# Product-key routing and one-hot batches in a two-layer decoder: where they stand, how they are laid out

## The chip, the cores and the metric

The kernel runs on one core of one Trainium2 chip. Its engines work side by side, each through its own queue of instructions in order: TensorE (PE, with its weight loads as PEld), VectorE (DVE), ScalarE (ACT), GpSimd (POOL) and SyncE (SP), which here only issues DMAs. They wait for each other by semaphores. The metric is the time on the device in microseconds (us), the median of several runs.

## What is computed

256 tokens of width 2048 pass two layers. Each ends with a PEER feed-forward part, which is what the change is about. Float32 throughout.

```python
def peer_ffn(h, w_q, keys_1, keys_2, expert_u, expert_v):
    q = (h @ w_q).reshape(b, s, PEER_HEADS, 2, PEER_HALF)          # 8 heads x 2 halves x 128
    s1 = jnp.einsum('bshd,hkd->bshk', q[..., 0, :], keys_1)        # 128 keys
    s2 = jnp.einsum('bshd,hkd->bshk', q[..., 1, :], keys_2)
    v1, i1 = lax.top_k(s1, 16)
    v2, i2 = lax.top_k(s2, 16)
    cand_sc = v1[..., :, None] + v2[..., None, :]                  # 256 candidates
    cand_id = i1[..., :, None] * 128 + i2[..., None, :]
    top_sc, pos = lax.top_k(cand_sc, 16)
    ids, g = cand_id[pos], softmax(top_sc)                         # 128 experts of 16384 per token
    act = gelu(expert_u[ids] @ h)
    return (g * act) @ expert_v[ids]
```

## The kernel before

**No gather.** The kernel runs over all 16384 experts. In the first pass of a layer 128 tiles of `expert_u` (128 experts each) are multiplied with the tokens and give the activations. In the second pass 128 tiles of `expert_v` are multiplied with activation times weight, where the weight of an expert that a token did not choose is zero. These dense weights come from the routing: for each token a matmul of one-hots, `hot2` (128 choices x second index) with `hot1g` (128 choices x first index, times g), gives a 128 x 128 block. g is split in two float16 parts, so each token has two matmuls of 128 columns (`build_w`, lines 1267 and 1268), and a batch of eight tokens has sixteen. There are 32 batches in a layer.

**Units.** All weights come through one stream of units of 128 x 2048 floats (1 MB). SP loads them into four raw slots (`load`, L348). ACT copies each half of a unit into `hi` (`split_hi`, L473), and DVE or POOL subtracts and gives `lo` (`split_lo`, L684 and L437), in a ring of four halves. Thus the hi of unit n+2 waits until TensorE is through with the same half of unit n. `gpsimd_takes` gives POOL one half of four, and three of four in the stretch of the routing. TensorE multiplies hi with both parts of the tokens (L1168) and lo with one (L1167), 32 matmuls for a unit of the projection or the first pass (`unit_a`), 24 of 512 columns for one of the second (`out_unit`, L1296, L1298, L1300). `unit_a` can run a piece of work, `middle`, between the two halves of a unit.

**Order on the engines.** It is written out by hand. A layer's PEER part is 16 units of projection (`routing`), 128 of the first pass (`peer`, index j) and 128 of the second (index t).
- In the projection DVE does for each unit u: the lo of unit u+2, the sum of unit u (`sum_halves`, L689, which frees the PSUM bank that unit u+2 needs), and the top 16 of unit u-1 (`route_unit`), whose keys product TensorE makes in the middle of unit u. Every second `route_unit` also makes the 256 candidates (L793) and their top 16.
- Tiles j = 0 to 6 of the first pass hold the last of these, then the decoding of the chosen places into indices (`decode`, L824, and `sum_places`, L834) and the softmax; at j = 7 TensorE transposes the selections and DVE stores them (`store_selections`).
- From j = 10 on, one tile in three carries a batch: DVE makes its one-hots behind the sum of tile j (L874 and L876, 24 instructions), TensorE multiplies them in the middle of tile j+1, and ACT copies the result into `w_stage` ahead of its work for tile j+2 (`stage_weights`, L557). Eight batches fill a stage, which SP stores in eight pieces of 512 KB, one every second tile (the last eight one in each tile).
- In the second pass four tiles are a group. For the next group DVE multiplies activation and weight (`weigh`, L882) at step i = 1, ACT copies this into `wa` (`coefficients_hi`, L566) at i = 2, and DVE subtracts (`coefficients_lo`, L886) at i = 3. Each stands on DVE behind the lo of unit t+2. TensorE waits for L886 ahead of the group's first matmul.

## Time and profile before

| | |
|---|---|
| median of 3 runs | 4781.25 us (4781.08 to 4782.48) |
| the profiled execution | 4780.19 us, its span 4778.5 us |
| TensorE busy | 4114.4 us, 86% of the span |
| VectorE, ScalarE, GpSimd busy | 48%, 37%, 20% |
| mean granted TensorE clock | 0.926 of full speed |
| DMA | 823 MB, mean 172 GB/s |

Matmuls are pipelined, so the starts of two of them give the pace, and busy time does not. "Idle before" is the time in which the engine had nothing to run, and the arrow names what ended it; "issue" is where the profile names nobody, as when the engine that was waited for had ended just before. A clock of 1.00 is 2.4 GHz, of 0.50 is 1.2; a window that holds both shows a value between.

### The profile page before, as it was taken

The page shows a single profiled execution, that of the slowest core. Times are in us where ns is not written, and L with a number is a line of the kernel's source. Part 1 is how long each engine was busy: PE and PEld are TensorE (multiplying, and loading weights), DVE is VectorE, ACT ScalarE, POOL GpSimd, SP SyncE. Part 2 cuts the span into 40 slices and gives each one's busy share as a digit, 9 for nine tenths or more (in the row PEclk, how much of TensorE's full clock was granted, in tenths as well). Part 3 has the DMA queues.
Part 4 walks back from the last instruction along what each step waited for, and adds up shares of the span by engine and source line. Part 5 has one row for each costly group of instructions (what it writes and reads, how often), then busy time and mean ns, then how long its engine had stood idle before and what let it go on. Part 6 is the DMA issues. An engine that isn't in the chain of part 4 may idle for free.

```text
span 4778.5 us, 50402 instructions
## 1 busy us (share of the span) xinstructions
PE 4114.4 (86%) x20142; PEld 3419.8 (72%) x20142; DVE 2312.9 (48%) x4301; ACT 1776.4 (37%) x2124; POOL 957.7 (20%) x422
## 2 busy tenths in 40 slices
PE   7988887788779999999898887887788998888887
PEld 6867766667667877777676776766667776666666
DVE  4444775555554444444446477555555433333333
ACT  3344333333334444434433423333333333333333
POOL 1232441111111222222110143111111111111111
PEclk9999998888889999999988999988888999999999
DMA  4533443455456766666432434445555765555553
GB/s 181 185 128 115 150 147 137 158 166 160 153 179 203 256 223 220 224 225 224 172 122 82 150 129 149 141 150 163 167 161 168 215 223 191 187 194 183 187 190 136
DMA packets 279163, 823.34 MB, mean 172 GB/s; under 512 B 146064, under 2 KB 178832, under 8 KB 195216
## 3 DMA queue, kind: packets, MB, share of 16 engines
q1 hardware_dynamic: 278496, 816.96, 50.0%
q8 instruction: 160, 2.62, 0.2%
q10 hardware_dynamic: 432, 3.15, 0.2%
q14 instruction: 75, 0.61, 0.0%
HBM read 750.84 MB, written 69.21 MB: 172 GB/s over the span
## 4 chain that ended last, share of the span: by engine, by line
PE 78%; DVE 9%; issue 9%; ACT 3%; POOL 0%; DMA 0%; DVEq 0%; SPq 0%; ACTq 0%; POOLq 0%
PE bank L1168 24%; PE bank L1167 12%; PE bank L1296 10%; PE bank L1300 10%; PE bank L1298 10%; PE bank L1188 2%; PE bank L1190 2%; DVE lo L684 2%; PE bank L1189 2%; ACT hi L473 2%; DVE wa L886 1%; PE bank L1267 1%; PE bank L1268 1%; DVE match L824 1%; PE bank L1170 1%
## 5 line engine op out<-in xcount | busy, mean ns | idle before, releaser
L473 ACT ACTIVATE hi<-raw 128x1024 fp32r<-128x1024 f32 x1294 | 1366.2, 1059 | 2440.4 <-PE bank L1168 1225.1
L684 DVE TENSOR_TENSOR lo<-raw,hi 128x1024 fp32r<-128x1024 f32 x919 | 1139.1, 1240 | 2077.4 <-ACT hi L473 2077.0
L1168 PE MATMUL bank<-act_t,hi 128*128 128x512 f32 x5120 | 1868.2, 411 | 23.2 <-DVE stage L689 17.7
L437 POOL TENSOR_TENSOR lo<-raw,hi 128x1024 fp32r<-128x1024 f32 x375 | 916.3, 2444 | 3746.5 <-ACT hi L473 3746.5
L1167 PE MATMUL bank<-act_t,lo 128*128 128x256 f32 x4800 | 1403.9, 292 | 0.0
L1168 PEld LDWEIGHTS bank<-act_t,hi 128*128 128x128 f32 x5120 | 990.1, 198 | 243.0 <-DVE stage L689 20.6
L1167 PEld LDWEIGHTS bank<-act_t,lo 128*128 128x128 f32 x4800 | 961.0, 200 | 13.5
L1296 PE MATMUL bank<-hi,wa 128*128 128x512 f32 x2048 | 672.3, 410 | 141.0 <-DVE wa L886 134.9
L1298 PE MATMUL bank<-lo,wa 128*128 128x512 f32 x2048 | 662.1, 405 | 0.0
L1300 PE MATMUL bank<-hi,wa 128*128 128x512 f32 x2048 | 661.5, 405 | 0.0
L1296 PEld LDWEIGHTS bank<-hi,wa 128*128 128x128 f32 x2048 | 393.5, 195 | 260.9 <-DVE wa L886 161.8
L1298 PEld LDWEIGHTS bank<-lo,wa 128*128 128x128 f32 x2048 | 397.1, 194 | 98.8
L1300 PEld LDWEIGHTS bank<-hi,wa 128*128 128x128 f32 x2048 | 396.3, 193 | 98.3
L1267 PE MATMUL bank<-hot1g,hot 128*128 128x128 f16 x512 | 112.5, 306 | 324.0 <-issue 313.8
L1267 PEld LDWEIGHTS bank<-hot1g,hot 128*128 128x128 f16 x512 | 72.7, 143 | 342.6 <-issue 342.6
L876 DVE TENSOR_SCALAR hot1g<-iota,sel_t 128x128 f16<-128x128 f16 x1024 | 275.6, 316 | 0.0
L689 DVE TENSOR_REDUCE stage<-bank 128x256 f32<-128x512 f32 x256 | 175.8, 687 | 177.9 <-PE bank L1168 174.3
L546 ACT ACTIVATE stage<-stage 128x256 f32<-128x256 f32 x256 | 105.7, 413 | 314.9 <-DVE stage L689 314.9
L874 DVE TENSOR_SCALAR hot<-iota,sel_t 128x128 f16<-128x128 f16 x512 | 198.5, 388 | 0.0
L1188 PE MATMUL bank<-hi,act_t 128*128 128x512 f32 x448 | 176.3, 394 | 3.7 <-DVE act_t L733 1.9
L1189 PE MATMUL bank<-lo,act_t 128*128 128x512 f32 x448 | 175.7, 392 | 0.0
L1190 PE MATMUL bank<-hi,act_t 128*128 128x512 f32 x448 | 175.6, 392 | 0.0
(208 smaller groups left out, 2348.4 us busy)
## 6 DMA issues: line engine op xcount, KB each, us to landing
raw<-in_stream SPq DMA_DIRECT2D x647, 1024.0 KB, 4.8
act_rows<-stage SPq DMA_DIRECT2D x64, 512.0 KB, 6.7
w_rows<-w_stage SPq DMA_DIRECT2D x64, 512.0 KB, 7.5
acts<-act_rows SPq DMA_DIRECT2D x64, 512.0 KB, 5.7
w_part<-w_rows SPq DMA_DIRECT2D x64, 512.0 KB, 6.7
x_res<-in_x SPq DMA_DIRECT2D x2, 1024.0 KB, 6.0
keys_sb<-in_keys ACTq DMA_DIRECT2D x2, 1024.0 KB, 4.8
out<-xn SPq DMA_DIRECT2D x2, 1024.0 KB, 4.0
```

The costliest lines, as they stand in the source:

```text
L437: pool.tensor_tensor(lo[:, s, :], raw[:, n0 % RAW_SLOTS, j * HALF:(j + 1) * HALF], hi[:, s, :].bitcast(F32), ALU.subtract).then_inc(lo_rea ...
L473: act.activation(hi[:, s, :], raw[:, slot, j * HALF:(j + 1) * HALF], ACT.Copy).then_inc(hi_ready[s], 1)
L684: dve.tensor_tensor(lo[:, s, :], raw[:, n0 % RAW_SLOTS, j * HALF:(j + 1) * HALF], hi[:, s, :].bitcast(F32), ALU.subtract).then_inc(lo_read ...
L876: ins = dve.tensor_scalar(hot1g[:, b % 2, t, w, :], iota[:], sel_t[:, 0, tok:tok + 1], sel_t[:, 2 + w, tok:tok + 1], ALU.is_equal, ALU.mult)
L1167: mm(ps[:, 0:S], w_lo, act_t[:, kt, 0, :], start=False, stop=False, skip_group_check=True)
L1168: ins = mm(ps[:], w_hi, act_t[:, kt, :, :].rearrange("p w t -> p (w t)"), start=first, stop=last)
L1188: mm(o, a_hi, w_hi, start=(kt == 0), stop=False)
L1189: mm(o, a_hi, w_lo, start=False, stop=False)
L1190: ins = mm(o, a_lo, w_hi, start=False, stop=(kt == kt_end - 1))
L1296: mm(o[:], a_hi, hi[:, s, at], start=first, stop=False)
L1298: mm(o[:], a_hi, lo[:, s, at], start=False, stop=False)
L1300: ins = mm(o[:], a_lo, hi[:, s, at], start=False, stop=last)
```

## The change

The routing is dealt over projection and first pass: TensorE's keys products stand in the middle of units i = 2, 3, 5, 6, 8, 9, ... (i counts from the projection's first unit), DVE takes the top 16 of the same unit's keys in these and the top 16 of a head's candidates in every third (`route_step`), then decoding takes units 26 to 39, and the selections are turned at unit 41 (j = 25). For this all sixteen projected units are kept (`pq_t`).

Batches begin at j = 26, two in every three tiles. The one-hots of eight tokens are made by four instructions on 1024 elements of float16, with the token as the innermost dimension. TensorE uses them three tiles later, reading each token's columns with a step of eight elements, and ACT stages the result one tile after that. Pieces of a stage are stored one per tile. GpSimd keeps its three halves of four up to j = 26. In the second pass `weigh`, `coefficients_hi` and `coefficients_lo` stand at i = 0, 1 and 2.

```diff
-BATCH_TILE = 10
-BATCH_STEP = 3
+BATCH_TILE = 26
+BUILD_LAG = 3
...
-TURN_TILE = 7
-EXP_TILE = 3
+ROUTE_AT = 2
+DECODE_AT = ROUTE_AT + 3 * 8
+TURN_AT = 41
+EXP_TILE = 12
...
-    b, off = divmod(tile - BATCH_TILE, BATCH_STEP)
-    return b if off == 0 and 0 <= b < BATCHES else None
+    three, r = divmod(tile - BATCH_TILE, 3)
+    b = 2 * three + r
+    return b if r < 2 and 0 <= b < BATCHES else None
+
+
+def last_batch_tile(f):
+
+    return BATCH_TILE + 3 * (FLUSH * (f + 1) - 1) // 2
...
-        pq_t = place("pq_t", 8, [P, 2, S])
+        pq_t = place("pq_t", 48, [P, 2 * PEER_HEADS, S])
...
+        g_full = place("g_full", 66, [P, S])
+        iota_rep = place("iota_rep", 67, [P, NKEYS, BATCH], F16)
+        hot1 = place("hot1", 69, [P, NKEYS, BATCH], F16)
+        hot2 = place("hot2", 71, [P, 2, NKEYS, BATCH], F16)
+        hot1g = place("hot1g", 75, [P, 2, 2, NKEYS, BATCH], F16)
...
-            busy = any(U0[f"wq{k}"] + LEAD <= n0 < U0[f"peer{k}"] + TURN_TILE + 3 + LEAD for k in range(2))
+            busy = any(U0[f"wq{k}"] + LEAD <= n0 < U0[f"peer{k}"] + BATCH_TILE + LEAD for k in range(2))
             return s >= 1 if busy else s == HALF_SLOTS - 1
...
-                    f, at = divmod(done - BATCH_TILE - 4, BATCH_STEP * FLUSH)
-                    piece, odd = divmod(at, 2 if f < FLUSHES else 1)
-                    if 1 <= f <= FLUSHES and piece < PIECES and odd == 0:
-                        store_weights(layer, f - 1, piece)
+                    f = next((f for f in range(FLUSHES) if 0 <= done - last_batch_tile(f) - BUILD_LAG - 3 < PIECES), None)
+                    if f is not None:
+                        store_weights(layer, f, done - last_batch_tile(f) - BUILD_LAG - 3)
...
-                    if batch_at(j - 2) is not None:
-                        stage_weights(batch_at(j - 2))
+                    b = batch_at(j - BUILD_LAG - 1)
+                    if b is not None:
+                        stage_weights(b)
                     split_hi(base + j + LEAD)
-                    if j == TILES - GROUP + 2:
+                    if j == TILES - GROUP + 1:
                         coefficients_hi(0)
                     gelu(j)
...
-                    if i == 2 and g + 1 < GROUPS:
+                    if i == 1 and g + 1 < GROUPS:
                         coefficients_hi(g + 1)
...
                 dve.wait_ge(c_full, idx + 1)
+                steps.sync()
                 top16(lambda c: ps_c[idx % 2][:, c * P:(c + 1) * P], lambda c: top_v[:, c, h, half, :],
...
+
+            def route_pairs(h):
+
                 steps.sync()
                 top16(lambda c: cand[:, c, :], lambda c: sel_v[:, c, h, :], lambda c: sel_p[:, c, h, :],
...
-                dve.tensor_copy(sel_t[:, 0:2, :].rearrange("p w t -> p (w t)"), ps_c[c0 % 2][:]).then_inc(c_free, 1)
+                dve.tensor_copy(i1_t[:], ps_c[c0 % 2][:, 0:S])
+                dve.tensor_copy(i2_t[:], ps_c[c0 % 2][:, S:2 * S]).then_inc(c_free, 1)
...
-                steps.do(dve.tensor_copy(g_half[:], g_full[:]))
-                steps.sync()
-                steps.do(dve.tensor_copy(sel_t[:, 2, :], g_half[:]))
-                steps.sync()
-                steps.do(dve.tensor_tensor(sel_t[:, 3, :], g_full[:], sel_t[:, 2, :], ALU.subtract))
-                steps.sync()
+                steps.do(dve.tensor_copy(g_parts[:, 0, :], g_full[:]))
+                steps.sync()
+                steps.do(dve.tensor_tensor(g_parts[:, 1, :], g_full[:], g_parts[:, 0, :], ALU.subtract))
+                steps.sync()
+
+            def route_step(layer, i):
+
+                n, r = divmod(i - ROUTE_AT, 3)
+                if 0 <= n < PEER_HEADS:
+                    if r < 2:
+                        route_unit(layer, 2 * n + r)
+                    else:
+                        route_pairs(n)
+                n = i - DECODE_AT
+                if n == 0:
+                    start_decoding(layer)
+                elif 1 <= n <= 12:
+                    w, r = divmod(n - 1, 6)
+                    if r < 4:
+                        decode(w, 4 * r, 4 * r + 4)
+                    else:
+                        sum_places(w, r - 4)
+                elif n == 13:
+                    finish_softmax(layer)
+                elif i == TURN_AT:
+                    store_selections(layer)
...
-                    if layer * BATCHES + b >= 2:
-                        dve.wait_ge(w_full, layer * BATCHES + b - 1)
-                    for t in range(BATCH):
-                        tok = BATCH * b + t
-                        dve.tensor_scalar(hot2[:, b % 2, t, :], iota[:], sel_t[:, 1, tok:tok + 1], None, ALU.is_equal)
-                        for w in range(2):
-                            ins = dve.tensor_scalar(hot1g[:, b % 2, t, w, :], iota[:], sel_t[:, 0, tok:tok + 1],
-                                                    sel_t[:, 2 + w, tok:tok + 1], ALU.is_equal, ALU.mult)
+                    done = layer * BATCHES + b
+                    tok = slice(BATCH * b, BATCH * (b + 1))
+                    if done >= 2:
+                        dve.wait_ge(w_full, done - 1)
+                    dve.tensor_tensor(hot2[:, b % 2, :, :], iota_rep[:],
+                                      i2_t[:, tok].unsqueeze(1).to_broadcast([P, NKEYS, BATCH]), ALU.is_equal)
+                    if done > 0:
+                        dve.wait_ge(hots_ready, done)
+                    dve.tensor_tensor(hot1[:], iota_rep[:], i1_t[:, tok].unsqueeze(1).to_broadcast([P, NKEYS, BATCH]),
+                                      ALU.is_equal).then_inc(hot1_ready, 1)
+                    dve.wait_ge(hot1_ready, done + 1)
+                    for w in range(2):
+                        ins = dve.tensor_tensor(hot1g[:, b % 2, w, :, :], hot1[:],
+                                                g_parts[:, w, tok].unsqueeze(1).to_broadcast([P, NKEYS, BATCH]), ALU.mult)
                     ins.then_inc(hots_ready, 1)
...
-                        if i == 1:
+                        if i == 0:
                             weigh(g + 1)
-                        elif i == 3:
+                        elif i == 2:
                             coefficients_lo(g + 1)
...
                     sum_tile(j)
...
+                    route_step(layer, 2 * PEER_HEADS + j)
                     if batch_at(j) is not None:
                         one_hots(batch_at(j))
...
+                steps.do(dve.tensor_copy(iota_rep[:], iota[:].unsqueeze(2).to_broadcast([P, NKEYS, BATCH])))
                 for u in range(2 * PEER_HEADS):
                     split_lo(w0 + u + LEAD)
-
-                    if C0[f"wq{layer}"] + u - 1 > 0:
-                        dve.wait_ge(c_full, C0[f"wq{layer}"] + u - 1)
                     unit_done(dve, w0 + u)
-                    sum_halves(pq_t[:, u % 2, :], a0 + u)
-                    if u >= 1:
-                        route_unit(layer, u - 1)
+                    sum_halves(pq_t[:, u, :], a0 + u)
+                    route_step(layer, u)
...
+            def key_unit(i):
+
+                n, r = divmod(i - ROUTE_AT, 3)
+                return 2 * n + r if r < 2 and 0 <= n < PEER_HEADS else None
...
-                        mm(o, hot2[:, b % 2, t, :], hot1g[:, b % 2, t, 0, :], start=True, stop=False)
-                        ins = mm(o, hot2[:, b % 2, t, :], hot1g[:, b % 2, t, 1, :], start=False, stop=True)
+                        mm(o, hot2[:, b % 2, :, t], hot1g[:, b % 2, 0, :, t], start=True, stop=False)
+                        ins = mm(o, hot2[:, b % 2, :, t], hot1g[:, b % 2, 1, :, t], start=False, stop=True)
...
+                    i, b = 2 * PEER_HEADS + j, batch_at(j - BUILD_LAG)
+                    middle = None
+                    if key_unit(i) is not None:
+                        middle = lambda u=key_unit(i): keys_product(layer, u)
+                    elif i == TURN_AT:
+                        middle = turn_selections
+                    elif b is not None:
+                        middle = lambda b=b: build_w(b)
+                    unit_a(base + j, a0 + j, middle=middle)
```

## Rows read from the trace of the kernel before

**Rows 1.** Windows: us; busy (x instructions) PE PEld DVE ACT POOL; PEclk, DMA, GB/s
```profile
686.80:1489.60 802.80, 640.72 (x3596) 556.75 (x3595) 423.95 (x1008) 290.57 (x353) 117.75 (x50) 0.89 0.50 159
...
1520.00:1560.00 40.00, 40.00 (x228) 34.75 (x227) 17.20 (x18) 17.47 (x22) 9.53 (x4) 1.00 1.01 274
...
1614.00:2363.00 749.00, 723.87 (x3068) 572.75 (x3069) 304.88 (x254) 300.11 (x286) 153.63 (x64) 1.00 0.61 221
...
3875.40:4763.00 887.60, 777.81 (x3068) 612.84 (x3069) 303.45 (x254) 298.27 (x285) 151.28 (x63) 0.93 0.51 183
```
**Rows 2.** Waits of the whole span: total us, times, longest us
```profile
PE bank L1267 <- issue: 313.8, 62, 5.1
...
PE bank L1296 <- DVE wa L886: 134.9, 62, 3.5
```
**Rows 3.** Timeline of TensorE, one batch of layer 0: start, length, idle before
```profile
801.10 0.27 PE L1267 MATMUL bank<-hot1g,hot 128*128 128x128 f16 x1 [5.11 <-issue]
...
802.72 0.56 PE L1167 MATMUL bank<-act_t,lo 128*128 128x256 f32 x1
```
**Rows 4.** Timeline of VectorE: first and last one-hots of that batch
```profile
796.04 0.25 DVE L874 TENSOR_SCALAR hot<-iota,sel_t 128x128 f16<-128x128 f16 x1
...
800.44 0.56 DVE L876 TENSOR_SCALAR hot1g<-iota,sel_t 128x128 f16<-128x128 f16 x2
```
**Rows 5.** Timeline of VectorE: sums of units, both layers
```profile
520.19 0.69 DVE L689 TENSOR_REDUCE pq_t<-bank 128x256 f32<-128x512 f32 x1 [5.32 <-PE bank L1168]
...
526.19 0.69 DVE L689 TENSOR_REDUCE pq_t<-bank 128x256 f32<-128x512 f32 x1 [0.91 <-PE bank L1168]
...
1566.95 0.69 DVE L689 TENSOR_REDUCE stage<-bank 128x256 f32<-128x512 f32 x1
...
1612.11 0.69 DVE L689 TENSOR_REDUCE stage<-bank 128x256 f32<-128x512 f32 x1
...
2753.12 0.69 DVE L689 TENSOR_REDUCE pq_t<-bank 128x256 f32<-128x512 f32 x1 [8.19 <-PE bank L1168]
...
3873.45 0.68 DVE L689 TENSOR_REDUCE stage<-bank 128x256 f32<-128x512 f32 x1
```
**Rows 6.** Timeline of TensorE: first matmul of output groups, first and last
```profile
1614.04 0.69 PE L1296 MATMUL bank<-hi,wa 128*128 128x512 f32 x2 [1.96 <-issue]
...
2341.48 0.72 PE L1296 MATMUL bank<-hi,wa 128*128 128x512 f32 x2 [0.81 <-DVE wa L886]
...
3875.37 0.70 PE L1296 MATMUL bank<-hi,wa 128*128 128x512 f32 x2 [4.18 <-issue]
...
4740.36 1.22 PE L1296 MATMUL bank<-hi,wa 128*128 128x512 f32 x2 [3.54 <-DVE wa L886]
```
**Rows 7.** Groups by line: count, busy us, mean ns of one, idle before
```profile
L557 ACT ACTIVATE w_stage<-bank 128x512 f32<-128x512 f32 x128 | 128.6, 1109 | 0.0
...
L882 DVE TENSOR_TENSOR acts<-acts,w_part 128x1024 f32<-128x1024 f32 x64 | 78.0, 1218 | 0.0
...
L834 DVE TENSOR_REDUCE sel_f<-match 128x128 f32<-128x2048 f32 x8 | 30.4, 3796 | 0.1
...
L503 ACT ACTIVATE xn<-x_res 128x512 f32<-128x512 f32 x32 | 19.9, 622 | 14.8 <-DVE x_res L950 7.6 <-DVE x_res L728 7.2
...
L699 DVE TENSOR_SCALAR xn<-x_res,stat 128x2048 f32<-128x2048 f32 x8 | 9.9, 1284 | 0.1
```
**Rows 8.** Timeline of GpSimd and VectorE beside each other, projection of layer 1
```profile
2788.68 2.38 POOL L437 TENSOR_TENSOR lo<-raw,hi 128x1024 fp32r<-128x1024 f32 x1 [3.66 <-ACT hi L473]
...
2789.83 2.31 DVE L684 TENSOR_TENSOR lo<-raw,hi 128x1024 fp32r<-128x1024 f32 x1
```
**Rows 9.** Timeline of VectorE: a pair step and a key step, layer 0
```profile
542.98 0.75 DVE L765 MAX8 sel_v<-cand 128x8 f32<-128x256 f32 x2
...
547.08 0.68 DVE L689 TENSOR_REDUCE pq_t<-bank 128x256 f32<-128x512 f32 x1
...
550.32 1.21 DVE L684 TENSOR_TENSOR lo<-raw,hi 128x1024 fp32r<-128x1024 f32 x1
```

More of the change, by code:

```diff
@@ L297, in build_program @@
         sel_t_ready = sem("sel_t_ready")
+        hot1_ready = sem("hot1_ready")
         hots_ready = sem("hots_ready")
@@ L1251, in keys_product, with routing @@
                 for c in range(NC_TOK):
-                    ins = mm(ps_c[idx % 2][:, c * P:(c + 1) * P], pq_t[:, u % 2, c * P:(c + 1) * P], keys_sb[:, u, :],
+                    ins = mm(ps_c[idx % 2][:, c * P:(c + 1) * P], pq_t[:, u, c * P:(c + 1) * P], keys_sb[:, u, :],
                              start=True, stop=True)
                 ins.then_inc(c_full, 1)
+            def key_unit(i):
+                n, r = divmod(i - ROUTE_AT, 3)
+                return 2 * n + r if r < 2 and 0 <= n < PEER_HEADS else None
+            def routing(layer):
+                for i in range(2 * PEER_HEADS):
+                    u = key_unit(i)
+                    unit_a(U0[f"wq{layer}"] + i, A0[f"wq{layer}"] + i,
+                           middle=(lambda u=u: keys_product(layer, u)) if u is not None else None)
             def peer(layer):
@@ L1303, in peer @@
                 for j in range(TILES):
-                    b = batch_at(j - 1)
-                    if j == 0:
-                        unit_a(base + j, a0 + j, middle=lambda: keys_product(layer, 2 * PEER_HEADS - 1))
-                    elif j == TURN_TILE:
-                        unit_a(base + j, a0 + j, middle=turn_selections)
-                    else:
-                        unit_a(base + j, a0 + j, middle=(lambda b=b: build_w(b)) if b is not None else None)
+                    i, b = 2 * PEER_HEADS + j, batch_at(j - BUILD_LAG)
[7 more added lines that the diff above has]
+                    unit_a(base + j, a0 + j, middle=middle)
                 pe.wait_ge(w_free, (layer + 1) * BATCHES)
@@ L1313, in peer @@
                     out_unit(t)
-            def routing(layer):
-                for u in range(2 * PEER_HEADS):
-                    unit_a(U0[f"wq{layer}"] + u, A0[f"wq{layer}"] + u,
-                           middle=(lambda u=u: keys_product(layer, u - 1)) if u else None)
             pe.wait_ge(consts, N_CONSTS)
```

38 lines of the change are left out of this document (4 added, 34 removed).

## The prediction

> **What bounds the kernel now.** I read the busy time by stage first [rows 1]. In the stretch in which batches of one-hots are made (686.8 to 1489.6 us, layer 0), TensorE is busy for 640.72 of 802.80 us at a granted clock of 0.89, and VectorE for only 423.95. No engine is full, so something is waited for. In a stretch without batches (1520 to 1560) TensorE is busy for 40.00 of 40.00 us at clock 1.00. Then the waits [rows 2]: TensorE stood 313.8 us in 62 waits ahead of L1267, the first matmul of a batch, and 134.9 us in 62 waits ahead of L1296, the first of a group of four output units. The order in time explains the first kind. VectorE's 24 one-hot instructions of a batch run from 796.04 to 801.00 [rows 4], and TensorE starts the batch at 801.10, 5.11 us idle [rows 3]. VectorE can begin a batch only behind the sum of a unit, and TensorE wants it in the middle of the very next unit. So TensorE's queue bounds the kernel, with holes that VectorE's latency makes, not its load. After the holes the clock falls to its lower level (1.2 of 2.4 GHz), which is the 0.89 and, in layer 1's output stage, the 0.93 [rows 1].
>
> **The pace without holes.** From 1566.95 to 1612.11 eight units pass [rows 5]: 45.16 / 8 = 5.645 us each. A unit with a keys product inside takes 526.19 - 520.19 = 6.00 us, so the product costs 0.36.
>
> **Projection and first pass, layer 0.** From the sum at 520.19 to the last at 1612.11 [rows 5] 142 units take 1091.92 us. The change leaves in this stretch: 142 x 5.645 = 801.6; 16 products x 0.36 = 5.8; 32 batches of 16 small matmuls, each 802.72 - 801.10 = 1.62 us [rows 3], 51.8; six transposes, about 1. Together 860.2, a saving of 231.7 us. Layer 1: 3873.45 - 2753.12 = 1120.33 us for 143 units; 807.2 + 5.8 + 51.8 + 1 = 865.8, a saving of 254.5.
>
> Why the holes should go:
> - Batches. One-hots of a batch now follow the sum of unit j and are used in the middle of unit j+3, not j+1: two units (11.3 us) more of room. The old hole was 5.1. The staging copy on ACT moves to j+4, where its semaphore is long up.
> - VectorE's load. A batch was 24 instructions in 4.96 us [rows 4]; it becomes four of 1024 two-byte elements, two SBUF inputs each. No row has that form. Bounds: 0.68 us (half of the 2048-element fp32 instruction L699, 1.284, plus a few hundredths) and 1.22 (L882, 1024 fp32 elements, two inputs) [rows 7]. A batch is then 2.7 to 4.9 us. I take 0.7 to 0.9: two-byte operands are nearer to the half rate. Two batches fall on three units: per six units VectorE has 9 halves of lo x 1.22 = 11.0, 6 sums x 0.69 = 4.1 and 4 batches, 10.8 to 19.5: 25.9 to 34.6 us, against TensorE's 6 x 5.645 + 4 x 1.62 = 40.4. Both ends are hidden, the upper one barely.
> - Routing. Sixteen key units and eight pair steps, formerly packed into the projection, now fall one to a unit over 24 units. The pair step takes 547.08 - 542.98 = 4.10 us, a key step with the sum 550.32 - 547.08 = 3.24 [rows 9]; with one lo per two units a period of three is about 3.24 + 4.0 + 4.8 + 1.5 x 1.22 = 13.9 of 16.9 us. Decoding becomes twelve steps; the heaviest are two sums of 3.80 us each in a row [rows 7], which with 2 x 0.69 and one lo fit into 11.3. The sum of unit j is wanted only at the start of j+2, so one step over 5.6 us is absorbed. The added steps.sync, the wait on hot1_ready (VectorE on its own write, with two multiplies queued behind it) and that on hots_ready (its own earlier batch, done) cost under 0.1 us each, in VectorE's slack. The exponential on ACT moves nine units later and is not awaited until unit 39.
> - GpSimd takes three halves of four for 42 units, not 26. A VectorE instruction with two SBUF inputs can be held by it: 2.31 us for a lo of 1.22 [rows 8], 1.09 too long. In two layers there are some 42 such lo in routing units: 0 to 46 us if all fell on the path. With the slack above I take 15.
> - SP's queue. The pieces of weights now leave one per unit for eight units out of every twelve, the acts stores and the loads behind them. The row of 1520 to 1560 is just such a stretch (the last flush already goes one per unit): DMA share 1.01, and TensorE never idle [rows 1]. Hidden by the ring of four raw slots; without it a landing late by one unit would cost 5.6.
>
> **The operands' layout.** The batch matmuls now read both operands with a step of eight two-byte elements, 16 bytes. No row shows a matmul with a step. Bounds per batch: 0.81 us, half of the 1.62 that stands in a stretch of low clock [rows 3], and about 3.2, twice it. The nearest row of a step that costs is ACT's copy L557, which writes 512 elements with a step: 1109 ns, against 622 for L503 without [rows 7], a factor of 1.8. Applied to the 0.81 this gives 1.5, so I keep 1.62.
> The Trainium skill (Advanced Engine Details and Errata, SBUF Cachelines) speaks against this part: lines of SBUF hold 16 bytes, and an access that goes to another line each time is penalised. It gives no figure; no run here shows it for TensorE.
> The Trainium skill (VectorE: DVE Perf Modes, The perf-mode tier table) gives tensor_tensor on two-byte data two elements a cycle, 1224 ns for 2048; an estimate from that is about 0.7 us for 1024, and by it the sum is the same, since VectorE is hidden either way.
>
> **Coefficients one unit up.** weigh, the ACT copy and the subtraction go from steps 1, 2, 3 of a group to 0, 1, 2. Now the subtraction stands behind the lo of the unit whose slot TensorE frees exactly when it reaches the group's end, hence 3.54 us in layer 1; in layer 0 GpSimd has that half, hence 0.81 [rows 6]. One unit earlier it is done some 2 us (5.66 - 3.54) before it is wanted. Its loads are issued at unit 4g for use at 4g+4, four units. Saving in layer 0: 31 x 0.81 = 25.1. In layer 1 the pitch of a group is (4740.36 - 3875.37) / 31 = 27.90 us; in layer 0 (2341.48 - 1614.04) / 31 = 23.47, less the hole 22.66, at clock 1.00. Saving 31 x 5.24 = 162.6, of which 110 are the hole and the rest the clock. The first groups' holes, 1.96 and 4.18, are 6 more.
>
> **Sum.** 231.7 + 254.5 + 25.1 + 162.6 + 6 = 679.9, less 15 = 665. The profiled execution took 4780.19 us (span 4778.5), 1 below the median; from the median 4781.25 I get 4116.
>
> **Rivals.**
> 1. The stepped operands cost nothing: 64 x 0.81 = 52 us less, 4064. For it: two-byte matmuls are short already. Against: the ACT rows.
> 2. They cost twice as much: 64 x 1.62 = 104 more, 4220. For and against: no row.
> 3. VectorE becomes the bound in the batch stretch, with 1.22 us for each instruction and GpSimd holding it three times in six units, 1.1 us each or the whole 2.38 of its instruction [rows 8]: 38 to 42 us against 40.4. Up to 1.5 us x 16 = 24 us, and the clock: holes of 3.5 us in 28 gave 0.93, 7% of 2 x 47 x 5.9 = 555 is 39. 4179. Against: fp32 is the wrong width.
> 4. The output stage keeps its hole, because the ACT copy now waits ahead of the hi of the next unit and delays it: 194 us stay, 4310. Against: ACT is busy 300 of 749 us there [rows 1].
> 5. Slower than before. One mechanism: the stepped reads in TensorE. It decides from 665 / 64 = 10.4 us on top of 1.62, 12 us per batch or 0.75 us per small matmul, over seven times the pitch of 0.10; at 0.8 us the time is 4116 + 64 x 11.2 = 4833. Nothing in the rows is near, but no row excludes it.
>
> **How the numbers follow.** The forecast (4080 to 4160) gets 0.58, rival 1 0.13, rival 2 0.10, rival 3 0.12, rival 4 0.03, rival 5 0.04. The likeliest is 4116. The range 4055 to 4225 takes in rivals 1 to 3, which leaves under 2 in 10 with the tails. A difference of 0.2% (10 us) is about what can be told from none. Faster 0.95, same 0.01, slower 0.04.
>
> **What would show it.** Waits ahead of the first batch matmul and of L1296's successor near zero; units in routing at 6.0 us; the batch stretch at clock 1.00 and over 97% TensorE; 22.7 us per output group in both layers. It is wrong if a batch takes over 3 us from its first matmul to the next unit's, if the one-hot instruction takes over 1.3 us, or if ACT waits for w_stored.

## The result and the profile after

The changed kernel took 4308.36 us (median of 4 runs, 4307.11 to 4309.1) against 4781.16 for the kernel before beside it: a ratio of 0.9011, interval 0.8995 to 0.9026, 473 us saved. The forecast was 4116 and the range ended at 4225. The direction was right, the size was not: 192 us of the expected gain are missing, and the time lies 88 us above rival 2's 4220. It is within 2 us of rival 4's 4310 as well, but by chance: that rival's mechanism isn't what happened, as the last part shows.

The engines' busy time in the kernel after:
```profile
PE 4156.2 (97%) x20142; PEld 3426.8 (80%) x20142; DVE 2155.2 (50%) x2991; ACT 1776.9 (41%) x2124; POOL 1027.0 (24%) x454
```
The longest sum of waits on TensorE in the kernel after (total us, times, longest), to be held against [rows 2]:
```profile
PE bank L1217 <- DVE xn L711: 43.6, 4, 19.1
```
Both waits that carried the old kernel are gone: TensorE waits neither ahead of L1291, the first matmul of a batch now, nor ahead of L1320, the first of an output group. What is left at the top of the list, 43.6 us in four waits, is the normalisation ahead of each attention and PEER part, and the kernel before had it too (43.5). So the holes closed as forecast, and the time went to something that isn't a wait.

The busy time by stage: batches of layer 0, first pass behind the batches, output stages of layers 0 and 1. Columns as in [rows 1].
```profile
763.00:1200.00 437.00, 437.00 (x2077) 349.46 (x2076) 234.61 (x252) 174.20 (x211) 58.95 (x25) 0.89 0.53 162
1200.00:1492.00 292.00, 292.00 (x1657) 253.66 (x1656) 130.48 (x131) 127.49 (x158) 61.81 (x26) 1.00 0.69 231
1494.00:2220.00 726.00, 715.08 (x3065) 574.01 (x3063) 313.00 (x265) 307.93 (x309) 155.19 (x65) 0.99 0.64 231
3578.00:4300.00 722.00, 713.23 (x3057) 572.62 (x3055) 310.96 (x262) 303.75 (x305) 151.20 (x63) 1.00 0.63 225
```
The first row is the clue: TensorE is busy for 437.00 of 437.00 us and yet its granted clock is 0.89, as it was with the holes [rows 1]. Weight loads take 349.46 of 437 (80%), against 87% in the row below. A busy share of 100% says nothing of the pace.

The sums of units on VectorE, as in [rows 5]: the second unit of the projection, unit 42 (the first one-hots are made behind its sum), the last; then the same for layer 1, from the first sum of the projection.
```profile
523.39 0.69 DVE L701 TENSOR_REDUCE pq_t<-bank 128x256 f32<-128x512 f32 x1 [4.87 <-PE bank L1181]
...
763.12 0.68 DVE L701 TENSOR_REDUCE stage<-bank 128x256 f32<-128x512 f32 x1
...
1492.32 0.69 DVE L701 TENSOR_REDUCE stage<-bank 128x256 f32<-128x512 f32 x1
...
2596.76 0.69 DVE L701 TENSOR_REDUCE pq_t<-bank 128x256 f32<-128x512 f32 x1 [7.47 <-PE bank L1181]
...
2839.81 0.69 DVE L701 TENSOR_REDUCE stage<-bank 128x256 f32<-128x512 f32 x1 [0.16 <-PE bank L1181]
...
3576.70 0.68 DVE L701 TENSOR_REDUCE stage<-bank 128x256 f32<-128x512 f32 x1
```
This splits each stretch. Routing: 763.12 - 523.39 = 239.7 us for 41 units (41 x 5.645 plus 16 products of 0.36 plus the transposes is 238.2) and 2839.81 - 2596.76 = 243.05 for 42 (243.9). It runs at the forecast pace. The other 101 units: 1492.32 - 763.12 = 729.2 and 3576.70 - 2839.81 = 736.9, where 101 x 5.645 = 570.1. That leaves 159.1 / 32 = **4.97 us** and 166.8 / 32 = **5.21 us** per batch, and the forecast had 1.62.

One batch on TensorE, to be held against [rows 3]: two matmuls of the unit before it, its first two, its last, and matmuls of the unit behind it; then the windows of the batch and of the stretch behind it, with the granted clock as the third number from the end.
```profile
905.90 0.40 PE L1181 MATMUL bank<-act_t,hi 128*128 128x512 f32 x1
...
906.25 0.40 PE L1181 MATMUL bank<-act_t,hi 128*128 128x512 f32 x1
906.49 0.43 PE L1291 MATMUL bank<-hot1g,hot 128*128 128x128 f16 x1
906.75 0.41 PE L1292 MATMUL bank<-hot1g,hot 128*128 128x128 f16 x1
...
910.02 0.41 PE L1292 MATMUL bank<-hot1g,hot 128*128 128x128 f16 x1
910.06 0.48 PE L1180 MATMUL bank<-act_t,lo 128*128 128x256 f32 x1
...
912.01 0.63 PE L1181 MATMUL bank<-act_t,hi 128*128 128x512 f32 x1
...
912.65 0.63 PE L1181 MATMUL bank<-act_t,hi 128*128 128x512 f32 x1
```
```profile
906.50:910.00 3.50, 3.50 (x16) 2.23 (x16) 1.23 (x1) 1.31 (x2) 1.47 (x1) 1.00 0.53 90
910.70:914.10 3.40, 3.40 (x13) 2.92 (x12) 0.00 (x0) 0.00 (x0) 0.00 (x0) 0.50 0.98 319
```
Two things can be read. The batch takes 910.06 - 906.49 = 3.57 us; from the second matmul to the last it is (910.02 - 906.75) / 14 = 0.2335 us from one to the next, where [rows 3] had 1.62 / 16 = 0.101, and that at the lower clock. Here the granted clock is 1.00 during the batch, so the slow pace isn't the clock's doing. And behind the batch a pair L1181 + L1180 takes 912.65 - 912.01 = 0.64 us; ahead of it the pair took 906.25 - 905.90 = 0.35. The clock is at its lower level there (0.50) for some 3.4 us, with no idle time before it fell: what TensorE did was 3.57 us of these matmuls.

### The profile page after: what moved, and what is told of

It reads as the page before. It is cut to its first block, busy times and chain, and to the rows that moved or that the text cites. A ratio compares the mean times of both kernels' runs of the same rounds, so it can differ in the third digit from the quotient of the medians.

```text
span 4305.4 us, 49124 instructions
## 1 busy us (share of the span) xinstructions
PE 4156.2 (97%) x20142; PEld 3426.8 (80%) x20142; DVE 2155.2 (50%) x2991; ACT 1776.9 (41%) x2124; POOL 1027.0 (24%) x454
## 4 chain that ended last, share of the span: by engine, by line
PE 94%; DVE 3%; issue 1%; ACT 1%; POOL 1%; DMA 0%; DVEq 0%; SPq 0%; POOLq 0%; ACTq 0%
PE bank L1181 29%; PE bank L1180 14%; PE bank L1320 11%; PE bank L1324 11%; PE bank L1322 11%; PE bank L1291 3%; PE bank L1292 3%; PE bank L1201 3%; PE bank L1202 3%; PE bank L1203 3%; PE bank L1183 1%; DVE lo L696 1%; PE bank L1217 1%; DVE act_t L722 0%; PE bank L1242 0%
## 5 line engine op out<-in xcount | busy, mean ns | idle before, releaser
L696 DVE TENSOR_TENSOR lo<-raw,hi 128x1024 fp32r<-128x1024 f32 x887 | 1091.9, 1232 | 1735.0 <-ACT hi L484 1733.8
L1181 PE MATMUL bank<-act_t,hi 128*128 128x512 f32 x5120 | 1869.9, 411 | 5.5 <-DVE act_t L722 5.5
L448 POOL TENSOR_TENSOR lo<-raw,hi 128x1024 fp32r<-128x1024 f32 x407 | 985.6, 2422 | 3204.1 <-ACT hi L484 3204.1
L1180 PE MATMUL bank<-act_t,lo 128*128 128x256 f32 x4800 | 1404.7, 293 | 0.0
L1181 PEld LDWEIGHTS bank<-act_t,hi 128*128 128x128 f32 x5120 | 988.0, 197 | 224.1 <-DVE act_t L722 6.7
L1180 PEld LDWEIGHTS bank<-act_t,lo 128*128 128x128 f32 x4800 | 957.4, 199 | 19.1
L1322 PE MATMUL bank<-lo,wa 128*128 128x512 f32 x2048 | 643.2, 395 | 0.0
L1324 PE MATMUL bank<-hi,wa 128*128 128x512 f32 x2048 | 643.2, 395 | 0.0
L1320 PE MATMUL bank<-hi,wa 128*128 128x512 f32 x2048 | 643.1, 395 | 0.0
L1322 PEld LDWEIGHTS bank<-lo,wa 128*128 128x128 f32 x2048 | 383.8, 187 | 94.1
L1324 PEld LDWEIGHTS bank<-hi,wa 128*128 128x128 f32 x2048 | 383.8, 187 | 94.0
L1320 PEld LDWEIGHTS bank<-hi,wa 128*128 128x128 f32 x2048 | 383.8, 187 | 93.9
L1291 PE MATMUL bank<-hot1g,hot 128*128 128x128 f16 x512 | 213.0, 416 | 0.0
L1292 PE MATMUL bank<-hot1g,hot 128*128 128x128 f16 x512 | 211.3, 413 | 0.0
L557 ACT ACTIVATE stage<-stage 128x256 f32<-128x256 f32 x256 | 104.8, 409 | 213.0 <-DVE stage L701 213.0
L568 ACT ACTIVATE w_stage<-bank 128x512 f32<-128x512 f32 x128 | 129.1, 1113 | 0.0
L915 DVE TENSOR_TENSOR hot<-iota_rep,i_t 128x1024 f16<-128x1024 f16 x64 | 112.5, 1759 | 0.0
```

What stands on the lines that cost most here:

```text
L448: pool.tensor_tensor(lo[:, s, :], raw[:, n0 % RAW_SLOTS, j * HALF:(j + 1) * HALF], hi[:, s, :].bitcast(F32), ALU.subtract).then_inc(lo_rea ...
L696: dve.tensor_tensor(lo[:, s, :], raw[:, n0 % RAW_SLOTS, j * HALF:(j + 1) * HALF], hi[:, s, :].bitcast(F32), ALU.subtract).then_inc(lo_read ...
L1180: mm(ps[:, 0:S], w_lo, act_t[:, kt, 0, :], start=False, stop=False, skip_group_check=True)
L1181: ins = mm(ps[:], w_hi, act_t[:, kt, :, :].rearrange("p w t -> p (w t)"), start=first, stop=last)
L1291: mm(o, hot2[:, b % 2, :, t], hot1g[:, b % 2, 0, :, t], start=True, stop=False)
L1292: ins = mm(o, hot2[:, b % 2, :, t], hot1g[:, b % 2, 1, :, t], start=False, stop=True)
```

## The experiments

The theory after the result: the missing time is the step of 16 bytes at which TensorE reads the one-hots, in two parts, the slow matmuls and the low clock behind them. The rivals: VectorE's load with GpSimd's holding (rival 3), something in the new order of routing, or a low clock that has another cause.

### The step of the operands

**step2**. The one-hots lie in pairs of tokens, so a matmul reads its 128 columns 4 bytes apart, not 16. VectorE's four instructions keep their size.
```
+SUB = 2
...
-        hot2 = place("hot2", 71, [P, 2, NKEYS, BATCH], F16)
-        hot1g = place("hot1g", 75, [P, 2, 2, NKEYS, BATCH], F16)
...
+        hot2 = place("hot2", 71, [P, 2, BATCH // SUB, NKEYS, SUB], F16)
+        hot1g = place("hot1g", 75, [P, 2, 2, BATCH // SUB, NKEYS, SUB], F16)
...
-                        mm(o, hot2[:, b % 2, :, t], hot1g[:, b % 2, 0, :, t], start=True, stop=False)
...
+                        mm(o, hot2[:, b % 2, t // SUB, :, t % SUB], hot1g[:, b % 2, 0, t // SUB, :, t % SUB], start=True, stop=False)
```


> The one-hots lie in pairs of tokens, so that TensorE reads columns 4 bytes apart, not 16. VectorE's four instructions keep two-byte rows of two tokens. Theory A (the 16-byte step of the operands makes each small matmul 0.234 us, and the low clock behind each batch comes from that): the small matmul falls to 0.10 us or less, the clock of the batch stretch goes to 1.00, and the six units of 54.6 us fall to about 40: 4308 - 64 x 3.6 = 4080 or less, down to 4030. Theory B (the small matmuls are slow because of where they stand, two batches in three units with VectorE writing beside them): pitch and time stay, 4300 to 4315.

**step4**. The same with SUB = 4: columns 8 bytes apart.

> The same with four tokens side by side: columns 8 bytes apart, two of them in 16 bytes. Theory A with a cost per 16 bytes touched: the small matmul stands between, 0.12 to 0.16 us, and the time near 4150 to 4200; if it is only the step of a whole 16 bytes that costs, the time is that of step2. Theory B: 4300 to 4315.

Measured: step2 4038.91 us (ratio 0.8445, 0.8431 to 0.8459), step4 4098.33 (0.8571, 0.8556 to 0.8585). The timeline of TensorE in step2, second and last matmul of a batch, and its window of batches:
```profile
907.47 0.22 PE L1296 MATMUL bank<-hot1g,hot 128*128 128x128 f16 x1
...
908.28 0.22 PE L1296 MATMUL bank<-hot1g,hot 128*128 128x128 f16 x1
```
```profile
763.00:1200.00 437.00, 437.00 (x2829) 381.68 (x2828) 290.36 (x310) 232.84 (x281) 87.13 (x36) 1.00 0.78 235
```
And in step4:
```profile
905.07 0.30 PE L1296 MATMUL bank<-hot1g,hot 128*128 128x128 f16 x1
...
906.72 0.29 PE L1296 MATMUL bank<-hot1g,hot 128*128 128x128 f16 x1
```
(908.28 - 907.47) / 14 = 0.058 us from one to the next, and (906.72 - 905.07) / 14 = 0.118. With 0.2335 at 16 bytes, the cost doubles with each doubling of the step. In step2 the clock is 1.00, and the same 437 us, with all 32 batches in either kernel, hold 2829 matmuls in place of 2077. Step2 is 269 us faster than the change and beats both kernels; nothing else was altered, so the order of routing and the lag are cleared. Step4 costs (4098.3 - 4038.9) / 64 = 0.93 us per batch over step2, and 16 x (0.118 - 0.058) = 0.96: at 8 bytes there is only the pitch (the time from one matmul to the next), no clock. I had expected 4150 to 4200 for it. At 16 bytes it is 269.5 / 64 = 4.21 us, of which 16 x (0.2335 - 0.058) = 2.81 are pitch, and 1.40 are left for the clock.

**Which operand.** stat_dense lays only the stationary operand (hot2) densely, mov_dense only the moving one (hot1g, with hot1).
```
-        hot2 = place("hot2", 71, [P, 2, NKEYS, BATCH], F16)
+        hot2 = place("hot2", 71, [P, 2, BATCH, NKEYS], F16)
```
```
-        hot1 = place("hot1", 69, [P, NKEYS, BATCH], F16)
-        hot1g = place("hot1g", 75, [P, 2, 2, NKEYS, BATCH], F16)
+        hot1 = place("hot1", 69, [P, BATCH, NKEYS], F16)
+        hot1g = place("hot1g", 75, [P, 2, 2, BATCH, NKEYS], F16)
```


> Only the stationary operand (hot2) lies dense, the moving one keeps its 16-byte step. Its one-hot instruction then reads a value repeated on the innermost dimension: 1.2 us for 0.68, so 0.6 us more on VectorE in a batch. If the stationary operand carries the cost: near step2's time. If the moving one does: 4300 to 4310. If both add: about half of step2's gain, near 4190.

> Only the moving operand (hot1g) lies dense, the stationary one keeps its 16-byte step. Three one-hot instructions at 1.2 us in place of 0.68. The mirror image of the run before: if the moving operand carries the cost, near step2's time plus at most 30 us of VectorE; if the stationary one, 4300 to 4310; if both add, near 4190.

Measured: stat_dense 4274.71 (0.894, 0.8926 to 0.8955), mov_dense 4044.99 (0.846, 0.8446 to 0.8474). Windows of the same stretch, stat_dense and then mov_dense:
```profile
840.00:1200.00 360.00, 360.00 (x1783) 278.20 (x1782) 204.71 (x207) 150.28 (x181) 57.61 (x21) 0.92 0.58 175
```
```profile
840.00:1200.00 360.00, 360.00 (x2290) 314.86 (x2289) 259.48 (x243) 189.56 (x228) 78.57 (x30) 1.00 0.81 242
```
The timeline of one batch: its second matmul and its last, in stat_dense and then in mov_dense.
```profile
903.63 0.41 PE L1292 MATMUL bank<-hot1g,hot 128*128 128x128 f16 x1
...
906.81 0.41 PE L1292 MATMUL bank<-hot1g,hot 128*128 128x128 f16 x1
```
```profile
905.65 0.23 PE L1293 MATMUL bank<-hot1g,hot 128*128 128x128 f16 x1
...
906.52 0.23 PE L1293 MATMUL bank<-hot1g,hot 128*128 128x128 f16 x1
```
With a dense stationary operand the pitch stays at (906.81 - 903.63) / 14 = 0.227; with a dense moving one it is (906.52 - 905.65) / 14 = 0.062. The step costs in the moving operand. The stationary one is still read at a step of 16 bytes in mov_dense, and its weight load takes 148 ns where step2's takes 97 (medians of the 512 of one line), but it overlaps the matmuls: mov_dense as a whole is only 6 us behind step2, though three of its four one-hot instructions on VectorE take 1.22 us. The stationary operand isn't quite free beside a slow moving one. stat_dense is 34 us faster than the change, where I had expected 4300 to 4310; its pitch accounts for 64 x 16 x (0.2335 - 0.227) = 7 of them, and its clock from 763 to 1200 us is 0.92, not 0.89. Why it is higher was not tried.

The Trainium skill (Advanced Engine Details and Errata, SBUF Cachelines) says that SBUF has lines of 16 bytes, that two hits on a line are needed to cover its latency, and that an access to another line each time is penalised. The runs agree on the direction. They differ on where it begins: at a step of 8 bytes two columns share a line and the pitch has doubled already, and the stationary operand's step shows in its weight load, which is hidden.

### The low clock

**split_batch**. The layout of the change, but a batch's 16 matmuls are put in two places of the unit: eight ahead of its first matmul, eight in its middle. Same matmuls, same step.
```
-                    for t in range(BATCH):
+                    for t in range(4 * part, 4 * part + 4):
...
-                        middle = lambda b=b: build_w(b)
-                    unit_a(base + j, a0 + j, middle=middle)
+                        head = lambda b=b: build_w(b, 0)
+                        middle = lambda b=b: build_w(b, 1)
+                    unit_a(base + j, a0 + j, middle=middle, head=head)
```


> The changed kernel with its 16-byte step, but the first eight matmuls of a batch stand ahead of the unit and the other eight in its middle, 1.87 us each time instead of 3.7 in one piece. The change costs 4.21 us per batch against step2 ((4308.4 - 4038.9) / 64), of which 16 x (0.2335 - 0.058) = 2.81 are the pitch and 1.40 the low clock behind it. If the clock falls because the slow reads stand in one piece, it stays at 1.00 and the time is 4308 - 64 x 1.4 = 4219. If it follows the mean rate of the stretch, nothing changes: 4300 to 4315.

Measured: 4219.19 (0.8824, 0.8809 to 0.8838). The timeline of a batch, first and last matmul of each part, and the window (the change itself has 0.87 for the clock in the same 360 us):
```profile
900.19 0.43 PE L1293 MATMUL bank<-hot1g,hot 128*128 128x128 f16 x1
...
901.84 0.41 PE L1294 MATMUL bank<-hot1g,hot 128*128 128x128 f16 x1
...
904.90 0.43 PE L1293 MATMUL bank<-hot1g,hot 128*128 128x128 f16 x1
...
906.55 0.41 PE L1294 MATMUL bank<-hot1g,hot 128*128 128x128 f16 x1
```
```profile
840.00:1200.00 360.00, 360.00 (x1905) 289.23 (x1904) 202.49 (x216) 162.71 (x193) 56.04 (x23) 1.00 0.64 190
```
The matmuls are as slow as before, 1.65 us from the first to the eighth in either part; the clock is 1.00 all along. The gain is (4308.4 - 4219.2) / 64 = 1.39 us per batch, the 1.40 that the subtraction above had left. So the low clock costs time, it comes of having the sixteen slow matmuls in one piece, and it is worth 89 us.

### VectorE as the bound

**both_dense**. Both operands dense: nothing stepped on TensorE, but the value per token is now the innermost repeated one on VectorE.
```
-                    dve.tensor_tensor(hot2[:, b % 2, :, :], iota_rep[:],
-                                      i2_t[:, tok].unsqueeze(1).to_broadcast([P, NKEYS, BATCH]), ALU.is_equal)
+                    dve.tensor_tensor(hot2[:, b % 2, :, :], iota[:].unsqueeze(1).to_broadcast([P, BATCH, NKEYS]),
+                                      i2_t[:, tok].unsqueeze(2).to_broadcast([P, BATCH, NKEYS]), ALU.is_equal)
```


> Both operands dense, all four one-hot instructions in the form that reads a value repeated on the innermost dimension. mov_dense measured 4045.0 and step2 4038.9. If the stationary operand's step costs nothing, the time is 4038 to 4060, VectorE having 0.5 us more in a batch and hiding it; if it costs a little, up to 10 us less than mov_dense. If VectorE is now the bound in the batch stretch (the rival of the prediction), TensorE shows waits ahead of the batch matmuls there and the time is above 4060.

**old_hots**. The change with the 24 small instructions per batch of the kernel before, at the new places and with the new lag.
```
+                    for t in range(BATCH):
+                        tok = BATCH * b + t
+                        dve.tensor_scalar(hot2[:, b % 2, t, :], iota[:], sel_t[:, 1, tok:tok + 1], None, ALU.is_equal)
+                        for w in range(2):
+                            ins = dve.tensor_scalar(hot1g[:, b % 2, t, w, :], iota[:], sel_t[:, 0, tok:tok + 1],
+                                                    sel_t[:, 2 + w, tok:tok + 1], ALU.is_equal, ALU.mult)
```


> The changed kernel with the 24 old one-hot instructions (dense, value as a scalar operand) in the new places. Theory A, the moving operand's step is the whole loss: 4035 to 4060, as both_dense, so the new form of the instructions gives nothing and the new places all. Rival: 24 short instructions, 4.96 us and more when GpSimd holds them, two batches in three units, make VectorE the bound: above 4080.

Measured: both_dense 4099.27 (0.8575, 0.856 to 0.859), old_hots 4106.8 (0.8592, 0.8577 to 0.8608). A wait, a window and a one-hot instruction of both_dense:
```profile
PE bank L1182 <- DVE stage L701: 43.4, 42, 1.8
```
```profile
820.00:1080.00 260.00, 243.80 (x1611) 208.16 (x1611) 240.47 (x196) 134.59 (x164) 49.85 (x19) 0.99 0.74 218
```
```profile
917.09 1.22 DVE L915 TENSOR_TENSOR hot<-iota,i_t 128x1024 f16<-128x1024 f16 x1
```
TensorE is fast here (pitch 0.056 in the trace) and waits for VectorE's sum instead: VectorE is busy for 240.47 of 260, TensorE for 243.80; old_hots has the same picture (241.63 and 243.09 of 260). Both missed what I expected of them, 4038 to 4060 and 4035 to 4060. That is rival 3 of the prediction, with the 1.22 us instruction that was its condition; it is 60 us slower than step2. mov_dense has three such instructions and one of 0.68 per batch and lost only 6 us: it stands just below the point at which VectorE becomes the bound.

**both_dense_act, dense_spread, spread_act.** Two ways to relieve VectorE in both_dense. dense_spread makes one batch in every two tiles rather than two in every three, in the layout of both_dense (`last_batch_tile`, not shown, follows). The `_act` forms let ACT make the hi copies ahead of the staging copy.
```
-    three, r = divmod(tile - BATCH_TILE, 3)
-    b = 2 * three + r
-    return b if r < 2 and 0 <= b < BATCHES else None
+    b, r = divmod(tile - BATCH_TILE, 2)
+    return b if r == 0 and 0 <= b < BATCHES else None
```


> both_dense (4099.3) with one batch in every two tiles instead of two in three, over tiles 26 to 88. Theory: both_dense lost its 54 us against mov_dense (4045.0) because VectorE, with four instructions of 1.22 us and GpSimd holding it, is the bound where two batches fall on three units. Per six units it then has 3 batches, not 4, 6 us less: TensorE's waits on the sum go, and the time is 4035 to 4050. If the dense stationary operand were the loss, it stays at 4090 to 4100.

> dense_spread (4179.4) with one order changed on ACT: the hi copies of unit j+2 first, then the staging of a batch. Theory, a chain in order of issue: the sum of a tile comes late behind the one-hots and the held lo, the gelu waits for the sum, the staging (1.8 us) and the hi copies stand behind the gelu, the next lo and sum wait for these; the pair of tiles takes 14.8 us where TensorE needs 12.2. Without the staging in the chain the pair takes 13.0: 64 x 1.8 = 113 us less, 4066. Rival, VectorE's own load is the bound: 4170 to 4180.

> both_dense (4099.3) with the same order on ACT. If the same chain is what cost it 54 us against mov_dense (4045.0), it falls to 4045 to 4070; if VectorE's load of 34.6 us and its waits for GpSimd in six units of 37.6 (6 x 5.645 + 4 x 0.93) are the bound, it stays above 4090.

Measured: dense_spread 4179.43 (0.874, 0.8725 to 0.8754), spread_act 4069.36 (0.851, 0.8495 to 0.8524), both_dense_act 4099.21 (0.8576, 0.8561 to 0.859). A wait and a window of dense_spread; then of spread_act; then the window of both_dense_act:
```profile
PE bank L1181 <- DVE stage L700: 101.8, 62, 2.5
```
```profile
820.00:1080.00 260.00, 227.04 (x1411) 193.52 (x1409) 204.61 (x161) 112.81 (x140) 58.83 (x18) 0.96 0.63 191
```
```profile
PE bank L1181 <- DVE stage L700: 18.5, 32, 0.7
```
```profile
820.00:1080.00 260.00, 248.28 (x1601) 212.01 (x1600) 230.64 (x181) 133.00 (x161) 64.52 (x20) 1.00 0.70 215
```
```profile
820.00:1080.00 260.00, 242.07 (x1610) 205.62 (x1608) 241.86 (x195) 135.74 (x163) 56.78 (x19) 1.00 0.74 219
```
My expectation of dense_spread fell. With less work per unit it became slower, and VectorE was busy for 204.61 of 260 only: it wasn't its load, but a chain. The timeline of dense_spread, VectorE and ACT:
```profile
904.70 0.68 DVE L700 TENSOR_REDUCE stage<-bank 128x256 f32<-128x512 f32 x1
...
905.41 0.42 ACT L556 ACTIVATE stage<-stage 128x256 f32<-128x256 f32 x1 [5.25 <-DVE stage L700]
905.74 1.98 ACT L567 ACTIVATE w_stage<-bank 128x512 f32<-128x512 f32 x2
907.51 2.00 ACT L483 ACTIVATE hi<-raw 128x1024 fp32r<-128x1024 f32 x2
908.61 2.36 DVE L695 TENSOR_TENSOR lo<-raw,hi 128x1024 fp32r<-128x1024 f32 x2 [3.23 <-ACT hi L483]
...
910.88 0.68 DVE L700 TENSOR_REDUCE stage<-bank 128x256 f32<-128x512 f32 x1
```
A sum ends at 905.38; ACT does the gelu, then two staging copies (1.98 us), and only then the hi; VectorE idles 3.23 us for it, makes two lo's, and comes to the next sum at 910.88. At one batch in two units, the staging falls on the same kind of unit each time, that in which VectorE has both halves of lo: in the trace the pattern repeats every 14.8 us, with 3.2 us of idle time each time. With the hi first (spread_act) the wait falls from 101.8 to 18.5 us and the time by 110. In both_dense the same edit changes nothing (4099.21 against 4099.27), and VectorE stays at 241.86 of 260: there it is the load. Two kernels with the same wait in the list (TensorE for the sum) had different causes, which VectorE's busy time told apart.

### The parts one by one

**coef_undone**. The change with the coefficients at their old places (ACT's copy goes back too).
```
-                        if i == 0:
+                        if i == 1:
...
-                        elif i == 2:
+                        elif i == 3:
```


> The changed kernel with weigh, the ACT copy and the subtraction back at steps 1, 2, 3. The prediction has the moved coefficients at 194 us: 4308 + 194 = 4502. If the clock in layer 1's output stage was low for another reason, only the holes come back, 25 + 110 + 6: 4449.

Measured: 4522.61 (0.946, 0.9443 to 0.9477), 214.2 us slower than the change. A wait and the window of layer 1's output stage:
```profile
PE bank L1320 <- DVE wa L929: 134.6, 62, 3.5
```
```profile
3610.00:4500.00 890.00, 776.10 (x3053) 611.33 (x3052) 305.60 (x255) 299.23 (x286) 151.19 (x63) 0.93 0.51 184
```
It is the old wait (134.9 in 62 in [rows 2]), with the old clock of 0.93.

**before_lag3**. The kernel before, with one thing changed: a batch is used three tiles behind its one-hots, not one.
```
-                    f, at = divmod(done - BATCH_TILE - 4, BATCH_STEP * FLUSH)
+                    f, at = divmod(done - BATCH_TILE - 6, BATCH_STEP * FLUSH)
...
-                    if batch_at(j - 2) is not None:
-                        stage_weights(batch_at(j - 2))
+                    if batch_at(j - 4) is not None:
+                        stage_weights(batch_at(j - 4))
...
-                    b = batch_at(j - 1)
+                    b = batch_at(j - 3)
```


> The kernel before with one edit: a batch is used by TensorE three tiles after it is made and staged in the fourth, still one batch in three tiles, old instructions, old routing, old coefficients. If the holes ahead of a batch and the low clock behind them are the whole loss of that stretch, its 25.1 us per three tiles fall to 17.8 to 18.6: 32 x 6.5 to 7.3 x 2 = 416 to 467 us, 4314 to 4365. If VectorE's 4.96 us still delay it: less than 300 us.

**lag3_coef**. before_lag3 with the coefficients one unit up as well.

> before_lag3 (4344.0) with the coefficients one unit up: everything of the change but the routing dealt out and the new form of one-hots. coef_undone puts the coefficients at 4522.6 - 4308.4 = 214 us, the prediction at 194: 4130 to 4150. What then lies between this kernel and step2 (4038.9) is the price of the routing as it stood: by the prediction's own terms (units of 6.3 to 8 us in projection and decoding against 5.65 to 6.0) about 90 to 110. If the two edits share their gain, by the clock, the time is above 4160.

Measured: before_lag3 4344.01 (0.9087, 0.9071 to 0.9103), lag3_coef 4132.48 (0.8641, 0.8627 to 0.8656). In the batch stretch of before_lag3 (710 to 1273 us) TensorE is busy for 555.42 of 563 us at a clock of 1.00, so the low clock of that stretch went with the holes. The window of lag3_coef in which the selections are decoded, in the first tiles of the first pass:
```profile
610.00:690.00 80.00, 63.80 (x337) 54.00 (x336) 66.54 (x130) 27.78 (x33) 37.73 (x16) 0.91 0.42 146
```
So the parts have these prices, each a difference of medians: the lag 4781 - 4344 = 437; the coefficients 211.5 (214.2 from the other side); dealing out the routing 4132.5 - 4106.8 = 26 (lag3_coef against old_hots); one-hots in four instructions 4106.8 - 4038.9 = 68 (old_hots against step2), if their layout costs TensorE nothing. With the layout of the change it costs 269.5 instead, so that part alone is a loss of 201.6. The five add up, as differences along one chain of kernels must: 4781.2 - 437 - 211.5 - 26 - 68 + 269.5 = 4308. The 26 are a net figure: TensorE's holes in the window above (16 us in layer 0) go, but since routing now takes up the first units of the pass, the batches behind it follow faster, two in three units, and with 24 instructions each TensorE waits for sums in old_hots as it does in both_dense (46.3 us in 40 waits). I had expected 90 to 110 us between lag3_coef and step2 for the routing alone; 94 was measured, but by luck, since 68 of them belong to the form of the one-hots.

## Why the prediction was wrong, step by step

**The batch's term failed.** It stood at 1.62 us, kept on the strength of one row, ACT's copy that writes with a step (a factor of 1.8). The factor was the wrong neighbour: another engine, and a write. It isn't the step's alone either, since L557 reads a PSUM bank and L503 reads SBUF. TensorE's moving operand measured 0.2335 against 0.058, a factor of 4. The batch measured 4.97 us in layer 0 and 5.21 in layer 1, which is 16 x 0.2335 = 3.74 plus 1.2 to 1.5 for the clock; the difference to 1.62 is 32 x 3.35 + 32 x 3.59 = 222 us, more than the whole miss of 192. From the pitch and split_batch alone it is 64 x (3.74 + 1.39 - 1.62) = 225. The prediction's own sign of being wrong, a batch of over 3 us from its first matmul to the next unit's, came true: 3.57.

**The bound of that term failed too.** I wrote that no row shows a matmul with a step and then took "twice as much" as the upper end, 3.24. Nothing in the rows supported 2. Rival 5 held the mechanism with its threshold, 12 us per batch, but nothing stood between 3.24 and 12, where the time then fell. A column at a step of 16 bytes spans eight times the bytes of a dense one; with that as the upper end a batch is up to 8 x 0.81 = 6.48 us, the time up to 4116 + 64 x 4.86 = 4427, and such a range, an estimate made afterwards, holds 4308. The prediction had named the Trainium skill's rule that speaks against this part (SBUF Cachelines, above), and gave it no price of its own; rivals 2 and 5, which carry the mechanism, took theirs from elsewhere.

**The clock had no term.** I charged the low clock to holes alone [rows 1], since every stretch with holes had it. The split shows it without any idle time, worth 1.39 us per batch.

**What held.** The holes: both waits went to zero. The pace of routing: 239.7 us against 238.2, and 243.05 against 243.9 (one term of VectorE's period there, the 4.0 us, has no row, but VectorE stayed hidden). The allowance of 15 us for GpSimd's holding was not needed: it happens, and the slack takes it. The one-hot instruction is at the lower end of its bounds, 0.68 us, and 2.9 when held, as the timeline of VectorE and GpSimd in the kernel after shows:
```profile
918.23 0.68 DVE L915 TENSOR_TENSOR hot<-iota_rep,i_t 128x1024 f16<-128x1024 f16 x1
...
926.73 2.43 POOL L448 TENSOR_TENSOR lo<-raw,hi 128x1024 fp32r<-128x1024 f32 x1 [18.76 <-ACT hi L484]
...
926.80 2.91 DVE L915 TENSOR_TENSOR hot<-iota_rep,i_t 128x1024 f16<-128x1024 f16 x1
```
SP's queue: TensorE is busy for 437.00 of 437.00 us in the batch stretch, so no load came late there. The coefficients: 214 against 194. A group takes 22.40 us, as between two of their subtractions here, where 22.66 was forecast; that is 62 x 0.26 = 16 of the 20 us:
```profile
1600.95 1.22 DVE L929 TENSOR_TENSOR wa<-acts,wa 128x1024 fp32r<-128x1024 f32 x1
...
1623.35 1.22 DVE L929 TENSOR_TENSOR wa<-acts,wa 128x1024 fp32r<-128x1024 f32 x1
```
The sum with measured terms: 679.9 - 222 + 16 = 474, and 473 was measured. The 222 come from the same trace, so this shows that no other large term is missing; their cause is shown by step2 and split_batch.

**The rivals.** Rival 1 was taken for an edge of the range, 4064; with a step that costs nothing the time is 4039 (step2), 25 lower than that. Rival 2 had the right mechanism and a size too small. Rival 3 isn't what happened, but it is real under its condition: both_dense has the 1.22 us instructions and waits for VectorE. Rival 4 gave 4310, the measured number within 2 us, and for a wrong reason: it had ACT delayed by its copy in the output stage and the hole kept. No such wait appears; the output stages run at clock 0.99 and 1.00, and coef_undone, which has the hole, takes 4523. A chain of the same kind, through ACT's staging copy, is real in dense_spread.

## What to carry to other kernels

Lay out a moving operand so that its columns lie next to each other, or at most 4 bytes apart for two-byte elements; put a step that another engine wants into the stationary operand, or pack the elements in pairs as step2 does, which keeps VectorE at 0.68 us and TensorE at 0.058 us a matmul, against 0.056 with both operands dense. Where no row shows an operation's form, don't borrow a factor from another engine: bound it by the bytes that each element touches. And read the pace of matmuls, or their number in a window, beside TensorE's busy time: at 437.00 of 437.00 us busy, 36% more matmuls fitted in.

## What was unexpected of the hardware

- A matmul of 128 float16 columns follows the last after 0.058 us with columns 4 bytes apart (0.056 dense), 0.118 at 8 bytes and 0.2335 at 16. It is the moving operand's step that counts: 0.062 with only the stationary one at 16 bytes, 0.227 with only the moving one.
- Sixteen of the slow matmuls in one piece (3.57 us) were followed by the lower level of the clock, with no idle time of TensorE; in two pieces of eight (1.65 us each, 3.06 us of other matmuls between them) the clock stayed at 1.00. What in them lowers it was not tried apart: step4's 16 matmuls take 1.8 us in one piece and leave it at 1.00 as well, so it may be their length or their pace.
- VectorE's instruction of 1024 two-byte elements takes 0.68 us when the innermost dimension of both inputs is read element by element, as in the change, and 1.22 when one value is repeated there, as in both_dense. The Trainium skill (VectorE: DVE Perf Modes, The perf-mode tier table) gives the first, by an estimate from its figure for 2048 elements, as 0.7; the rows agree.
